# A linear-attention recurrence between dense blocks: tile order, PSUM banks of the state updates, and where the intra products stand

## The reference, cut to what matters

```python
q_dec = q * exp(b);  k_tail = k * exp(b_last - b)          # b: running sum of log f in a chunk
scores = einsum('nbhid,nbhjd->nbhij', q_dec, k_inv) * causal
o_intra = einsum('nbhij,nbhjv->nbhiv', scores, v)
def step(state, xs):
    o_c = einsum('bhid,bhdv->bhiv', q_c, state)             # "inter"
    state = state * decay[..., None] + einsum('bhjd,bhjv->bhdv', k_c, v_c)   # "update"
    return state, o_c
o_a = rms_norm(o_intra + o_inter, out_norm) * sigmoid(g)
o_b = gate_b * causal_depthwise_conv(gate_c * h_b, conv_w)
mix = concatenate([o_a, o_b]) @ w_out
```

## Time and profile before

| | |
|---|---|
| median of 3 runs | 1170.58 us |
| span of the profiled execution | 1167.9 us |
| blocks C, H, B with the recurrence | 119.6 to 216.1 us |
| out0 starts | 217.8 us |
| TensorE busy | 1142.4 us, 98% |
| VectorE / ScalarE busy | 895.6 us, 77% / 753.0 us, 64% |

### The profile page before, as it was taken

How to read it: one execution, slowest core, us unless ns; L and a number is a source line. 1 busy time by engine, 2 the same in 40 slices (tenths; PEclk the granted TensorE clock), 3 DMA queues, 4 the chain that set the end, 5 groups by cost and what they waited for, 6 DMA issues and landing times.

```text
span 1167.9 us, 17158 instructions
## 1 busy us (share of the span) xinstructions
PE 1142.4 (98%) x5862; PEld 904.9 (77%) x5862; DVE 895.6 (77%) x1233; ACT 753.0 (64%) x960; POOL 131.6 (11%) x91
## 2 busy tenths in 40 slices
PE   9999999999999999999999999999999999999996
PEld 7778777875888888888788875675888888888775
DVE  6542447737999999999886449836999999999886
ACT  7563231335878878788765439735778788788765
POOL 0000000001112212121000000001112122121000
PEclk9999999999999999999999999999999999999999
DMA  9652222333899999999772320323899999999731
GB/s 367 250 229 73 73 72 73 114 115 116 321 361 380 390 376 376 378 372 392 269 308 72 109 72 1 121 99 124 299 350 388 380 382 381 377 375 383 271 144 72
DMA packets 50596, 286.30 MB, mean 245 GB/s; under 512 B 9321, under 2 KB 9597, under 8 KB 21358
## 3 DMA queue, kind: packets, MB, share of 16 engines
q1 hardware_dynamic: 37086, 250.93, 56.1%
q0 software_dynamic: 13456, 34.65, 8.1%
HBM read 271.38 MB, written 30.41 MB: 258 GB/s over the span
## 4 chain that ended last, share of the span: by engine, by line
PE 87%; DVE 6%; ACT 3%; DMA 1%; issue 1%; ACTq 0%; DVEq 0%; POOLq 0%
PE psum L564 82%; PE psum L967 2%; DVE arena L2680 2%; ACT whi L1409 1%; DMA arena<-vscr,cur 1%; DVE arena L2693 1%; PE psum L1008 1%; ACT ahi L1409 1%; PE psum L878 1%; DVE wlo L1984 0%; DVE h L2513 0%; DVE h L2520 0%; DVE wlo L1980 0%; ACT arena L1409 0%; DVE h L2506 0%
## 5 line engine op out<-in xcount | busy, mean ns | idle before, releaser
L1980 DVE TENSOR_TENSOR wlo<-raw,whi 128x2048 fp32r<-128x2048 f32 x200 | 456.3, 2290 | 68.4 <-ACT whi L1409 55.2
L564 PE MATMUL psum<-whi,ahi 128*128 128x512 f32 (+1 forms) x1184 | 467.9, 397 | 3.3 <-ACT ahi L1409 2.8
L564 PE MATMUL psum<-wlo,ahi 128*128 128x512 f32 (+1 forms) x1184 | 456.4, 387 | 0.8 <-DVE wlo L1984 0.8
L564 PE MATMUL psum<-whi,alo 128*128 128x512 f32 (+1 forms) x1184 | 451.9, 387 | 0.0
L1409 ACT ACTIVATE whi<-raw 128x2048 fp32r<-128x2048 f32 x200 | 382.8, 1916 | 42.6 <-PE psum L564 42.6
L564 PEld LDWEIGHTS psum<-whi,ahi 128*128 128x128 f32 x1184 | 222.5, 188 | 52.4 <-issue 5.3
L564 PEld LDWEIGHTS psum<-whi,alo 128*128 128x128 f32 x1184 | 222.3, 188 | 46.1
L564 PEld LDWEIGHTS psum<-wlo,ahi 128*128 128x128 f32 x1184 | 222.6, 188 | 42.2 <-DVE wlo L1984 1.3
L1409 ACT ACTIVATE arena<-psum 128x512 f32<-128x512 f32 (+3 forms) x150 | 83.1, 565 | 123.5 <-PE psum L564 99.1
L1409 ACT ACTIVATE ahi<-psum 128x512 fp32r<-128x512 f32 x146 | 82.1, 593 | 86.4 <-PE psum L967 39.3
L564 PE MATMUL psum<-arena 32*128 32x128 f32 (+9 forms) x818 | 115.7, 330 | 0.9 <-ACT arena L1409 0.8
(11 more groups left out here) (221 smaller groups left out, 907.5 us busy)
## 6 DMA issues: line engine op xcount, KB each, us to landing
raw<-w_moe_dram SPq DMA_DIRECT2D x192, 1024.0 KB, 8.8
raw<-w_dense_dram SPq DMA_DIRECT2D x34, 1024.0 KB, 8.8
yscr<-arena POOLq DMA_DIRECT2D x2, 4096.0 KB, 23.2
arena<-yscr SPq DMA_DIRECT2D x6, 1024.0 KB, 6.7
vscr<-arena POOLq DMA_DIRECT2D x8, 512.0 KB, 2.9
h<-x_dram SPq DMA_DIRECT2D x4, 512.0 KB, 7.9
arena<-w_proj_dram POOLq DMA_DIRECT2D x2, 1024.0 KB, 6.8
arena<-yscr SPq DMA_DIRECT2D x4, 512.0 KB, 4.5
```

Source lines behind the costliest of these rows:

```text
L564: return nc.tensor.matmul(o, l, r, start=start, stop=stop, **kw)
L1980: tt(wlo[:, b % SPL, :], raw[:, b % RAW, :], halves(whi[:, b % SPL, :]), ALU.subtract).then_inc(lo_ready, 1)
```

## The change

Three things change for blocks C, H and B. The tiles go in ROWS order, and q uses bank q % 2, so that banks 2 to 5 are free; `pair_read` gives the waits that this needs on the banks' former readers. The updates of all heads of a step go to four banks (2 to 5) in one group, with one `g_U`, and the second round with its wait is gone. The intra products of all four heads of a block of 128 tokens stand together ahead of every fourth step (r = 0, 4, 8, 12). In the programs of ScalarE and VectorE the splits, copies, roots, convolutions and gates are put where the new order makes their input ready: in each block the second chunk of the next block is split at the last tile (j = 7), `conv(q)` comes at the even tiles of B and `gate(q)` at the odd ones. The diff, without the hunk in `gate`, which only takes its bank from `bank`:

```diff
--- before.py
+++ after.py
@@ -336,15 +336,24 @@
             return (ORDER[n] * TB + tb) * 2 + half + 1
 
 
-        READ = {1: (g_sig, 0), 2: (g_silu, 0), 3: (g_v, 0), 4: (g_g, 0), 5: (g_C, 0),
-                6: (g_H, 0), 7: (g_ob, 0), 8: (s_add, 0), 10: (M[0]["gt"], 0),
+        READ = {1: (g_sig, 0), 2: (g_silu, 0), 3: (g_v, 0), 8: (s_add, 0), 10: (M[0]["gt"], 0),
                 11: (M[0]["gt"], 4), 12: (t_z, 0), 15: (s_add, 4),
                 17: (M[1]["gt"], 0)}
 
         def bank(k, q):
 
+            if k in (BLK["C"], BLK["H"], BLK["B"]):
+                return PS[q % 2]
             return PS[(q + 2) % 4] if k in (BLK["out1"], BLK["out1"] + 1) else PS[q]
 
+        def pair_read(k, q):
+
+            if k == BLK["out0"]:
+                return g_ob, (3, 4, 3, 4)[q]
+            if q >= 2:
+                return {BLK["C"]: g_C, BLK["H"]: g_H, BLK["B"]: g_ob}[k], q - 1
+            return {BLK["C"]: (g_g, q + 1), BLK["H"]: (g_C, q + 3), BLK["B"]: (g_H, q + 3)}[k]
+
         def nhalf(tb, half):
 
             return (ORDER[3] * 2 + half) * TB + tb + 1
@@ -355,18 +364,13 @@
 
             return [hh for hh in range(HEADS) if 0 <= r - hh < NCH - 1]
 
-        def rounds_U(r):
-
-            pairs = [[hh for hh in heads_U(r) if hh // 2 == j] for j in range(2)]
-            return [p for p in pairs if p]
-
         def done_U(r):
 
-            return sum(len(rounds_U(j)) for j in range(r + 1))
+            return sum(1 for j in range(r + 1) if heads_U(j))
 
         def U_bank(hh):
 
-            return PS[4 + hh % 2][:, hh * P:(hh + 1) * P]
+            return PS[2 + hh][:, 0:P]
 
         def out_bank(tb):
 
@@ -624,6 +628,8 @@
 
             def bank_read(k, q):
 
+                if BLK["C"] <= k <= BLK["out0"]:
+                    pe.wait_ge(*pair_read(k, q))
                 if k in READ:
                     pe.wait_ge(READ[k][0], READ[k][1] + q + 1)
                 if k == BLK["aq1"]:
@@ -790,12 +796,14 @@
                 return mm(U_bank(hh), Kt[rows, tb, hh * P:(hh + 1) * P],
                           V[rows, tb, hh * P:(hh + 1) * P], True, True)
 
-            def intra(tb, hh):
-
-                if hh == 0 and tb >= 2:
+            def intra(tb):
+
+                if tb >= 2:
                     pe.wait_ge(g_o, tb - 1)
-                return mm(out_bank(tb)[:, hh * P:(hh + 1) * P], ST[:, tb, hh * P:(hh + 1) * P],
-                          V[:, tb, hh * P:(hh + 1) * P], hh == 0, False, skip_group_check=True)
+                for hh in range(HEADS):
+                    last = mm(out_bank(tb)[:, hh * P:(hh + 1) * P], ST[:, tb, hh * P:(hh + 1) * P],
+                       V[:, tb, hh * P:(hh + 1) * P], hh == 0, False, skip_group_check=True)
+                return last
 
             def inter(n, hh):
 
@@ -814,28 +822,27 @@
                     pe.wait_ge(g_v, TB)
                     pe.wait_ge(g_ktail, TB)
                     pe.wait_ge(g_scm, TB)
+                    pe.wait_ge(g_g, TB)
+                if r % CPB == 0 and r < NCH:
+                    last = intra(r // CPB)
+                    if r == 0:
+                        last.then_inc(g_in, 1)
                 pe.wait_ge(g_S, r + 1)
-                rounds = rounds_U(r)
-                if rounds:
-                    for hh in rounds[0]:
+                if heads_U(r):
+                    for hh in heads_U(r):
                         last = update(r, hh)
                     last.then_inc(g_U, 1)
-                hh = r % CPB
-                if r - hh < NCH:
-                    last = intra((r - hh) // CPB, hh)
+                if r == 0:
+                    return
                 for hh in range(HEADS):
                     if 0 < r - hh < NCH:
                         last = inter(r - hh, hh)
                 last.then_inc(g_in, 1)
-                if len(rounds) > 1:
-                    pe.wait_ge(g_U, done_U(r) - 1)
-                    for hh in rounds[1]:
-                        last = update(r, hh)
-                    last.then_inc(g_U, 1)
 
             pe.wait_ge(g_S, 1)
             for b, name in enumerate("CHB"):
-                dense(BLK[name], "w", after=lambda i, q, b=b: rec(b * 8 + i * 4 + q))
+                dense(BLK[name], "w", order=ROWS,
+                      after=lambda i, q, b=b: rec(b * 8 + q * 2 + i))
 
             def oa_T(tb):
 
@@ -1613,25 +1620,25 @@
 
 
             splits(11)
-            splits(12)
             for q in range(4):
+                if q == 3:
+                    splits(12)
+                    out_rows(0)
                 group_done(act, BLK["C"], q)
                 if q == 0:
                     act.wait_ge(g_qdec, TB)
-                copy(E[:, q, :], PS[q][:, :]).then_inc(g_C, 1)
-                if q == 0:
-                    out_rows(0)
+                copy(E[:, q, :], bank(BLK["C"], q)[:, :]).then_inc(g_C, 1)
             splits(13)
             out_root(0)
             out_rows(1)
+            out_root(1)
             splits(14)
-            out_root(1)
             out_rows(2)
             splits(15)
             out_root(2)
             out_rows(3)
+            out_root(3)
             splits(16)
-            out_root(3)
 
             def conv_hi(tb):
 
@@ -2223,23 +2231,24 @@
                    hc("triI").unsqueeze(1).to_broadcast([P, HEADS, P]), ALU.mult)\
                     .then_inc(g_scm, 1)
             splits(10)
-            for b in range(3):
-                for i in range(2):
-                    for q in range(4):
-                        if i == 1 and b == 1:
-                            group_done(dve, BLK["H"], q)
-                            dve.wait_ge(g_C, q + 1)
-                            tt(E[:, q, :], PS[q][:, :], E[:, q, :], ALU.mult).then_inc(g_H, 1)
-                        if i == 0 and b == 2 and q >= 1:
-                            conv(q - 1)
-                        if i == 1 and b == 2:
-                            gate(q)
-                            if q == 0:
-                                conv(3)
-                        if b * 8 + i * 4 + q < 21:
-                            rec(b * 8 + i * 4 + q)
-                        if q == 0:
-                            splits(first_chunk(BLK["C"] + b) + i + 3)
+            for b, name in enumerate("CHB"):
+                for j in range(8):
+                    q, i = j // 2, j % 2
+                    if j == 7:
+                        splits(first_chunk(BLK[name]) + 4)
+                    if i == 1 and name == "H":
+                        group_done(dve, BLK["H"], q)
+                        dve.wait_ge(g_C, q + 1)
+                        tt(E[:, q, :], bank(BLK["H"], q)[:, :], E[:, q, :], ALU.mult)\
+                            .then_inc(g_H, 1)
+                    if i == 0 and name == "B":
+                        conv(q)
+                    if i == 1 and name == "B":
+                        gate(q)
+                    if b * 8 + j < 21:
+                        rec(b * 8 + j)
+                    if j == 0:
+                        splits(first_chunk(BLK[name]) + 3)
 
             def conv_lo(tb):
 
```

More of the change, by code:

```diff
@@ L2214, in gate @@
                 group_done(dve, BLK["B"], ft)
-                tt(E[:, ft, :], PS[ft][:, :], conv_out(ft), ALU.mult).then_inc(g_ob, 1)
+                tt(E[:, ft, :], bank(BLK["B"], ft)[:, :], conv_out(ft), ALU.mult)\
+                    .then_inc(g_ob, 1)
             splits(8)
```

## The result

The changed kernel takes 1162.59 us (median of 4 runs, 1162.22 to 1163.84) against 1170.59 us before; the ratio is 0.9937, 95% interval 0.9925 to 0.9949. The forecast was 1162.8 us. The profiled execution has a span of 1160.5 us, 2.1 us under its own time, where 1160.1 was forecast.

A forecast was written before the change was run, and what follows sets the result against it. TensorE's own instruction sequence was taken as the bound. Steps -9.4 and gap +1.6 gave -7.8 us: span 1167.9 to 1160.1, plus 2.7 made 1162.8 us (chance 0.70); range 1161.0 to 1167.0.

The forecast's parts named there:

- Plain step 3.72 us, third and fourth update free: Recurrence steps without intras in blocks C, H, B: period 3.72 us instead of 4.60, with updates three and four adding nothing.
- Intra step 4.62: Steps 4, 8 and 12, with four grouped intra products: period 3.72 + 0.90 = 4.62 us, no shorter than before.
- Sum of the steps -9.4: Steps 0 to 17 together: 70.15 us instead of 79.52, a gain of 9.4 us.
- The gap +1.6: TensorE's gap between block B's end and out0: last gate queued behind VectorE's late split of chunk 15, 1.6 us lost.
- Thin cover 0.4 us at step 17: VectorE's update of step 16 ends at 10.8 us, TensorE wants it at 11.2: covered by 0.4 us, no wait.
- What follows is shifted as a whole: Everything after out0 starts keeps its length, 950.1 us, and only moves in time; later SP loads cost nothing.
- 2.7 us around the span: Median run time lies 2.7 us above the profiled execution's span, kept unchanged and added to the forecast span of 1160.1.
- The clock: Clock drop in the longer gap ahead of out0 (about 2.3 us without matmuls): no row prices it, left in the tails.
- B: Rival, in the steps: third and fourth update queue behind the first two, +4.2 us, 1167.0 us; chance 0.12.
- D: Rival, steps 2 to 15: the four updates take turns, each with its own weights, 11.6 us, 1174.4 us; chance 0.03.
- C: Rival, around block changes: VectorE becomes the bound, covers at steps 16 and 17 fail, TensorE waits 1 to 3 us, 1165; chance 0.10.
- E: Rival, behind the stage: it ends sooner but TensorE waits later for something that didn't move, 1170.6 us; chance 0.05.

## Why the prediction was right, and where it wasn't

- **TensorE's list bounds the stage**: right. It was filled before, and afterwards its only wait in it and behind it up to out0 is the 2.21 us.
- **Plain step 3.72 us, third and fourth update free**: 3.74 measured; the updates twice over show that the row groups work side by side. The Trainium skill's 3.07 times for four row tiles (TensorE: Matmul & The Clock Gate, Part 3: Packing small matmuls) would by my estimate have made it some 0.09 us dearer; the step is 0.04 us longer than step 17 with one update and two inters (3.70), so here it is at most half of that. The page's figure is for 512 columns, these products have 128.
- **Intra step 4.62**: steps 3 and 4 together 8.40 against 8.34 forecast; step 0 4.34 against 4.23.
- **Sum of the steps -9.4**: -8.9 (79.52 - 70.58). The 0.4 us missing are 0.02 in most plain steps and the rest in the four steps with intras.
- **The gap +1.6**: +1.54 (3.24 - 1.70), and by the mechanism named: with the gate ahead it is gone.
- **Thin cover 0.4 us at step 17**: right (189.16 - 188.76), and 1.5 us more work there turned into a wait of 1.17.
- **What follows is shifted as a whole**: 950.3 against 950.1 us. SP's later loads cost at most those 0.2.
- **2.7 us around the span**: 2.1 around this one. The 2.7 set the median of three executions against the span of another; every execution with both on record, before and changed, lies 1.8 to 2.3 us above its own span. This error of 0.6 us gave back what the steps lacked, so it is luck that the total is nearer to the forecast than its terms are.
- **The clock**: this is the step that failed, a term put at nothing. I saw the longer gap, wrote that no row prices a fall of the clock, and left it in the tails. Of the changed kernel's 14 executions 4 lie at 1162.05 to 1162.59 and 10 at 1163.84 to 1165.12; the mean clock is 0.998 in all 4 and 0.996 in all 10, and the two profiles of that second group both show the clock at half for about 3.4 us behind the gap. The likeliest time of this kernel is therefore about 1164.2, not 1162.8. It stays in the range only because the range was made for another case (B), which didn't happen. The first four runs held one of the long executions (1163.84) and three short ones, so their median shows none of it.

The rivals: B and D fell with the plain period of 3.74 us and the updates twice over, C with the cover that held, E with the 950.3 us. By parts, then: fewer shapes -8.9, the gap +1.5, and in most executions the clock behind the gap another +1.6 or somewhat more. With the gate first the last two are gone (1161.15 us), and with the gate in two parts the kernel is at 1160.60 us.

## What to carry to other kernels

Count the array shapes that small products make TensorE go through, not the products: here a second group for the same four update instructions cost 0.41 us, an intra product alone 0.45 against 0.23 in a group of four, and a further product in another row or column group of the same shape 0.02 at most. So group them by shape. Each row group wrote to a bank of its own here, and no run shows that it may be otherwise, so keep them apart. When a tile order is changed, ask which weight slot comes free later and what stands behind that split in its engine's list. A wait of TensorE costs more than its length once the clock falls behind it (2.21 us of wait, and 1.6 us more), so a new gap of about 2 us is worth removing or filling, and worth more than four runs to judge.

## What the runs showed of the hardware that I had not expected

A wait of 2.21 us, behind transposes of 1.03 us, brought the granted clock from 2.4 to 1.2 GHz in 10 of 14 executions, as far as their times and mean clocks tell (seen in two profiles of those, and not in the one profile of the others), for some 3.4 us and 1.6 us of time. Among the experiments with the same wait, two of five profiles show it too (one intra in each step, longer convolution), three don't. A wait of 4.38 us did so in the one profile taken, already within the wait, and lifted all six times; it cost 2.5 us beside its length (8.10 instead of 5.57 us to the next transposes). Waits of 0.33, 0.66 and 0.73 us did not. The one wait of 1.17 us (the longer convolution) left the clock at 1.00 right behind it. 28 matmuls whose result nobody reads, 1.73 us in all, put into the gap, kept the clock up and took the 1.6 us away without moving anything else. Whether the transposes ahead of the wait matter for the clock was not tested.
